# A hybrid diffusion trunk step on one core: the xBC and step-size projection in three rounded products

## The reference, cut to what matters

```
h = modulate(rmsnorm(x, n1), sh1, sc1)               # (384, 1024)
a_q,a_k,a_v, b_q,b_k,b_v, z, xbc, dt_raw = split(h @ w_in)   # w_in (1024, 2320)
xbc = silu(conv_centred(xbc, conv_w, conv_b))        # 768 columns, 3 taps along tokens
dt = softplus(dt_raw + dt_bias)                      # 16 columns
... attention of two kinds, Mamba-2 scan on xbc, dt, z -> o
x = x + g1 * (o @ w_out)
x = x + g2 * moe(modulate(rmsnorm(x, n2), sh2, sc2)) # 16 experts, top 2 in the top group
```

## Time and profile before

| | |
|---|---|
| runs | 819.34, 819.86, 821.42 us (median 819.86) |
| profiled execution | 819.76 us, its span 817.9 us |
| PE busy | 758.9 us, 93% of the span |
| DVE busy | 586.0 us, 72% |
| ACT busy | 476.9 us, 58% |
| chain that ended last | PE 79%, DVE 11%, ACT 5% |
| L825, plain product | 69.2 us in 192 records |

### The profile page before, as it was taken

How to read it: one execution, slowest core, us unless ns; L and a number is a source line. 1 busy time by engine, 2 the same in 40 slices (tenths; PEclk the granted TensorE clock), 3 DMA queues, 4 the chain that set the end, 5 groups by cost and what they waited for, 6 DMA issues and landing times.

```text
span 817.9 us, 10722 instructions
## 1 busy us (share of the span) xinstructions
PE 758.9 (93%) x3980; PEld 571.8 (70%) x3980; DVE 586.0 (72%) x934; ACT 476.9 (58%) x768; POOL 49.7 (6%) x36
## 2 busy tenths in 40 slices
PE   4997989999989999999989998988997799999995
PEld 2565878457945888888766787745793688888874
DVE  4229676884558789999663866688544988999965
ACT  3033883575355777777542388357534687777752
POOL 0000641000000000000000064100000000000000
PEclk9999999999999999999999999999998999999998
DMA  9952032978347899999760113285830179999912
GB/s 368 422 186 75 30 128 60 419 294 310 104 155 308 289 374 358 372 363 370 270 273 12 58 46 129 104 339 177 303 109 0 52 268 377 357 376 371 360 51 80
DMA packets 33488, 185.98 MB, mean 227 GB/s; under 512 B 5136, under 2 KB 6288, under 8 KB 16400
## 3 DMA queue, kind: packets, MB, share of 16 engines
q1 hardware_dynamic: 33424, 185.16, 60.2%
HBM read 182.53 MB, written 2.62 MB: 226 GB/s over the span
## 4 chain that ended last, share of the span: by engine, by line
PE 79%; DVE 11%; ACT 5%; issue 4%; DMA 1%; DVEq 0%; SPq 0%; ACTq 0%
PE psum L739 22%; PE psum L854 11%; PE psum L768 11%; PE psum L1056 8%; PE psum L825 7%; PE psum L791 3%; PE psum L620 2%; PE psum L1070 1%; DVE att L1930 1%; PE psum L817 1%; PE psum L924 1%; PE psum L717 1%; PE psum L1026 1%; PE psum L661 1%; PE psum L752 1%
## 5 line engine op out<-in xcount | busy, mean ns | idle before, releaser
L1726 DVE TENSOR_TENSOR split<-ring,split 128x2048 fp32r<-128x2048 f32 x96 | 219.9, 2291 | 27.6 <-ACT split L1319 25.0
L1319 ACT CAST split<-ring 128x2048 fp32r<-128x2048 f32 x96 | 183.4, 1911 | 18.1 <-PE psum L768 14.5
L739 PE MATMUL psum<-split,y_hi 128*128 128x512 f32 x512 | 162.7, 399 | 0.0
L739 PEld LDWEIGHTS psum<-split,y_hi 128*128 128x128 f32 x512 | 93.7, 188 | 19.6
L739 PE MATMUL psum<-split,y_lo 128*128 128x512 f32 x256 | 100.6, 393 | 0.0
L854 PE MATMUL psum<-ring_r,hT_hi 128*128 128x512 f32 x216 | 74.0, 397 | 2.7 <-ACT qkT L1413 2.4
L768 PE MATMUL psum<-split,hidT 128*128 128x512 f32 x256 | 70.3, 396 | 1.8 <-DVE hidT_lo L1731 1.8
L825 PE MATMUL psum<-hT,ring 128*128 128x384 f32 x192 | 69.2, 499 | 0.0
L768 PEld LDWEIGHTS psum<-split,hidT 128*128 128x128 f32 x256 | 47.4, 187 | 14.5 <-DVE hidT_lo L1731 3.6
L2120 POOL TENSOR_TENSOR ud<-const,da_hi 128x1024 fp32r<-128x1024 f32 x12 | 30.7, 2578 | 431.8 <-DVE da_lo L1823 431.3
L739 PEld LDWEIGHTS psum<-split,y_lo 128*128 128x128 f32 x256 | 48.0, 188 | 11.1
(11 more groups left out here) (258 smaller groups left out, 1339.0 us busy)
## 6 DMA issues: line engine op xcount, KB each, us to landing
ring<-in_w_gu SPq DMA_DIRECT2D x64, 1024.0 KB, 5.0
ring<-in_w_ada SPq DMA_DIRECT2D x40, 1024.0 KB, 6.7
ring<-in_w_down SPq DMA_DIRECT2D x32, 1024.0 KB, 5.2
ring<-in_w_rows SPq DMA_DIRECT2D x12, 1024.0 KB, 5.1
ring<-in_first SPq DMA_DIRECT2D x8, 1024.0 KB, 14.7
ring<-in_w_out SPq DMA_DIRECT2D x8, 1024.0 KB, 4.8
ring<-in_w_xbc SPq DMA_DIRECT2D x8, 784.0 KB, 8.4
par<-in_par SPq DMA_DIRECT2D x1, 1632.0 KB, 11.9
```

Of the source, the lines that this page charges most:

```text
L739: last = pe.matmul(dst, x[:, g, t, :], w[:, j, :], start=(t == 0 and i == 0), stop=(t == KD - 1 and i == 2))
L1319: act.copy(splits[n % SPLITS][:, 0, :], slot(key)).then_inc(raised("whi", l, p), 1)
L1726: tt(lo, slot(unit_key(l, p, n)), hi.bitcast(F32), ALU.subtract).then_inc(raised("wlo", l, p), 1)
```

## The change

The xBC and step-size product is made in three rounded products. Parts:

1. Per chunk 18 products (weight high x h high, weight rest x h high, weight high x h rest, for six groups) in place of 6 plain ones. Step sizes: h high against the 32 columns of dt_w (high and rest side by side), and h rest against the 16 high ones, six in place of three; VectorE adds the two results after the bias, one more add behind L1777.
2. The high part of x's pieces goes to new tiles x_hi and dt_w; the rest overwrites the piece. Pair 0 is split whole by VectorE at the start of the norm (the high part too), pairs 1 to 3 by ScalarE and VectorE in turn.
3. h is split chunk by chunk (`split_h`) within the norm in place of halves after it.
4. hT_hi has ring slots 2 and 3 for itself from the beginning of the stage: the h_hi entries stand first in the list, and the xbc pieces go elsewhere.
5. In layer 0 the casts of constant tables (`tables`) come after chunk 5, and the splits of w0 and w1 after chunk 6, both inside the norm; ScalarE's copies of the modulation rows are interleaved with the splits. w2 is split after the first convolution group. In layer 1 w0 and w1 are split after x3.

```diff
+IN_ORDER = (("x0", "h0", "h1", "x1", "h2", "h3", "x2", "h4", "h5", "x3", "h6", "w0", "w1", "h7", "w2", "w3", "w4", "w5"),
+            ("x0", "h0", "h1", "h2", "h3", "x1", "h4", "h5", "h6", "h7", "x2", "x3", "w0", "w1", "w2", "w3", "w4", "w5"))
...
-    s = [("norm", 0)] + ada[:early] + [("w_split", 0), ("h_split", 0), ("w_split", 1), ("h_split", 1), ("w_split", 2), ("xbc",)]
+    s = [("norm", 0)] + ada[:early] + [("xbc",)]
...
             if s[0] == "xbc":
+                pieces += [("h_hi", l, 0), ("h_hi", l, 1)]
                 if l == 0:
                     pieces.append(("first", 0, 0))
...
-        elif key[0] == "xbc" and key[2] < 2:
-            b = H_AT + 1 - key[2]
+        elif key[0] == "h_hi":
+            b = H_AT + key[2]
...
+        if key[0] == "h_hi":
+            last_use[b] = pieces.index(("w_hi", key[1], 5)) - 0.2 + 0.1 * key[2]
...
+                x_hi = sb("x_hi", [P, KD, XBC], F32R, c=ahead_of_masks)
+                dt_w = sb("dt_w", [P, KD, 2 * DT], F32R, c=ahead_of_masks)
...
 TensorE, kind "xbc"
-                            pe.wait_ge(*landed(("xbc", l, i)))
+                            pe.wait_ge(*in_lo(l, f"x{i}"))
                             for kk in range(2):
                                 k = 2 * i + kk
-                                pe.wait_ge(*modulated(l, 0, k))
+                                pe.wait_ge(*in_lo(l, f"h{k}"))
                                 for m in range(TILES):
-                                    last = pe.matmul(dtd[:, m * DT:(m + 1) * DT], hT[:, k, m * P:(m + 1) * P],
-                                                     w[:, kk, XBC:XBC + DT], start=(k == 0 and m == 0),
+                                    pe.matmul(dtd[:, 2 * m * DT:2 * (m + 1) * DT], hT_hi[:, k, tok], dt_w[:, k, :],
+                                              start=(k == 0 and m == 0), stop=(k == KD - 1), skip_group_check=True)
+                                    last = pe.matmul(dtd[:, 2 * m * DT:(2 * m + 1) * DT], hT_lo[:, k, tok], dt_w[:, k, 0:DT],
...
-                                    last = pe.matmul(bank(("xbc", l, c))[:, 0:TOK], w[:, kk, c * P:(c + 1) * P], hT[:, k, :],
-                                                     start=(k == 0), stop=(k == KD - 1))
+                                    for j, (w, x) in enumerate(((x_hi[:, k, part], hT_hi), (x_lo(l, i)[:, kk, part], hT_hi),
+                                                                (x_hi[:, k, part], hT_lo))):
+                                        last = pe.matmul(bank(("xbc", l, c))[:, 0:TOK], w, x[:, k, :],
...
 ScalarE
+            def split_x(l, i):
+                act.wait_ge(*landed(("xbc", l, i)))
+                act.copy(x_hi[:, 2 * i:2 * i + 2, :], src[:, :, 0:XBC])
+                act.copy(dt_w[:, 2 * i:2 * i + 2, 0:DT], src[:, :, XBC:XBC + DT]).then_inc(sig["in_hi"], 1)
+            def split_h(l, k):
+                act.wait_ge(*modulated(l, 0, k))
+                act.copy(hT_hi[:, k, :], hT[:, k, :]).then_inc(sig["in_hi"], 1)
...
 ScalarE, norm of layer 1 (c over all chunks; odd ones are modulated here)
+                    if not n:
+                        split_h(l, c)
+                        if c == 3:
+                            split_x(l, 1)
...
 ScalarE, kind "xbc"
                         if l == 0:
                             for j in range(KD):
                                 key = ("first", 0, j)
                                 act.wait_ge(*full(key))
                                 act.copy(ada_rows[:, 0:2 * P], bank(key)[:, 0:2 * P]).then_inc(*was_read(key))
+                                split_h(0, j)
+                                if j % 2 and j < KD - 1:
+                                    split_x(0, (j + 1) // 2)
+                                if j == KD - 2:
+                                    for p in range(2):
+                                        split_win(0, p)
...
+                        else:
+                            split_x(l, 2)
+                            split_x(l, 3)
+                        for p in range(0 if l else 2, 3):
+                            split_win(l, p)
...
 VectorE, norm
+                if l < DEPTH and not n:
+                    dve.wait_ge(*landed(("xbc", l, 0)))
+                    dve.tensor_copy(x_hi[:, 0:2, :], src[:, :, 0:XBC])
+                    dve.tensor_copy(dt_w[:, 0:2, 0:DT], src[:, :, XBC:XBC + DT]).then_inc(dve_step, 1)
+                    dve.wait_ge(dve_step, dve_steps())
+                    split_x(l, 0)
                 dve.wait_ge(sig["rstd"], 2 * l + n + 1)
...
+                    if l and not n and c0 == 1:
+                        split_h(l, 0)
...
+                        if not (l or n):
+                            split_h(0, c)
+                            if c % 2 and c < KD - 1:
+                                split_x(0, (c + 1) // 2)
+                            if c == KD - 3:
+                                tables()
+                            if c == KD - 2:
+                                for p in range(2):
+                                    split_win(0, p)
+                    if l and not n and c0:
+                        for c in range(c0, c1):
+                            split_h(l, c)
+                        for i in (1,) if c0 == 1 else (2, 3):
+                            split_x(l, i)
...
 VectorE, kind "xbc"
+                        for p in range(2 if l else 0):
+                            split_win(l, p)
...
+                        tt(dt_in, both[:, 0], bias, ALU.add).then_inc(dve_step, 1)
+                        dve.wait_ge(dve_step, dve_steps())
+                        tt(dt_in, both[:, 1], dt_in, ALU.add).then_inc(*was_read(key))
...
-                            if c == 2:
-                                dve.wait_ge(*release["xbc", l, KD // 2 - 1])
-                                split_h(l, 1, KD - 2, KD)
+                            if c == 0:
+                                split_win(l, 2)
```

More of the change, by code:

```diff
@@ L261, in build @@
                         pieces += [("first", 0, j) for j in (2 * i + 1, 2 * i + 2) if j < KD]
-                pieces += [("win", l, p) for p in range(5)] + [("w_hi", l, 2), ("win", l, 5), ("w_hi", l, 4), ("h_hi", l, 0),
-                                                               ("h_hi", l, 1), ("w_hi", l, 5)]
+                pieces += [("win", l, p) for p in range(5)] + [("w_hi", l, 2), ("win", l, 5), ("w_hi", l, 4), ("w_hi", l, 5)]
             elif s[0] == "ada":
@@ L404, in build @@
             cbd = sb("cbd", [P, 2], c=mix)
+            with ExitStack() as ahead_of_masks:
+                x_hi = sb("x_hi", [P, KD, XBC], F32R, c=ahead_of_masks)
+                dt_w = sb("dt_w", [P, KD, 2 * DT], F32R, c=ahead_of_masks)
             with ExitStack() as shared_late:
@@ L1229, in out_hi @@
                 act.copy(splits[out_split(n)][:, 0, :], slot(("wout", l, n))).then_inc(sig["mhi"], 1)
+            def split_x(l, i):
+                act.wait_ge(*landed(("xbc", l, i)))
+                src = slot(("xbc", l, i))[:, 0:2 * (XBC + DT)].rearrange("p (k n) -> p k n", k=2)
+                act.copy(x_hi[:, 2 * i:2 * i + 2, :], src[:, :, 0:XBC])
+                act.copy(dt_w[:, 2 * i:2 * i + 2, 0:DT], src[:, :, XBC:XBC + DT]).then_inc(sig["in_hi"], 1)
+            def split_h(l, k):
+                if k == 0:
+                    for i in range(2):
+                        if former_in["h_hi", l, i]:
+                            act.wait_ge(*release[former_in["h_hi", l, i]])
+                act.wait_ge(*modulated(l, 0, k))
+                act.copy(hT_hi[:, k, :], hT[:, k, :]).then_inc(sig["in_hi"], 1)
             def split_win(l, p):
@@ L1348, in _ @@
                         norm(l, arg[0])
-                        if not (l or arg[0]):
+                    elif kind == "ada" and arg[2] == KD - 1:
+                        ada(arg[0], arg[1])
+                    elif kind == "w_split":
+                        split_win(l, arg[0])
+                    elif kind == "xbc":
+                        if l == 0:
                             for j in range(KD):
```

98 lines of the change are left out of this document (46 added, 52 removed).

## The result

The changed kernel takes 826.94 us (median of 7 runs, 822.78 to 827.5), the kernel before 820.24 us on the same chip: ratio 1.0069, with a 95% interval of 1.005 to 1.0088. The change makes it 0.7% slower. The prediction was 809.3 us, range 803.5 to 816, with 0.89 for faster; it is wrong in sign. The profiled execution took 827.36 us (span 825.5, before 817.9).

What follows compares the result with a forecast made beforehand. TensorE's matmuls were taken to pace both products, except 4.29 us idle before layer 0's rows. From 819.8 us, less 6.9 in layer 0 and 3.6 in layer 1, came 809.3 us, range 803.5 to 816.

Steps and rivals of the forecast that it cites:

- Part 1: Product itself: wide fp32r products at 0.174 us, narrow ones at 0.095 us; a chunk takes 3.70 us in layer 1.
- Rival B: Both layers' products: narrow step products cost a wide one's 0.174 us each; 814 us; chance 0.08.
- Parts 2 to 4: Layer 0's feeding, ring and rows: product gains 1.3 us after 4.1 us of waits, rows start at 63.3; gain 6.9 us.
- Part 5: Layer 1's product: starts at 425.2, gains 6.7 us less waits of 1.7 and 1.4, ends at 456.4; gain 3.6 us.
- Rival D: Layer 0, chunk 5 into the rows: clock falls to half in waits; 30 us of it makes 824 us; chance 0.07.
- parts 3 to 5: Layer 0's ring and rows, layer 1's product: waits of 4.1 us in layer 0, 1.7 and 1.4 us in layer 1.
- the 4.29 us: Idle between product and first row product of layer 0 in the kernel before; the clock fall after it cost 1.3 us.
- Rival A: Feeding slower, above all in layer 0 around x3, w0, w1 and last modulation row: 812 to 814 us; chance 0.22.
- Rival C: Waits shorter in both layers as VectorE and ScalarE run ahead; all of 4.1 + 1.4 us back: 804 us; chance 0.12.
- Rival E: Rows wait for VectorE's convolution behind w2's split, both layers; 6 us of delay makes about 818 us; chance 0.06.
- Part 6: Layer 0's attention: nothing taken, bounds 0.9 us either way; experts, output product and end untouched.

Runs made afterwards that it cites:

- the combination with the root in SBUF: Changed kernel with layer 1's first norm root in SBUF, x0's split behind chunk 0's modulation in layer 1, and const and par loads moved: 818.04 us, 0.9968.
- the best version: the combination with the root in SBUF plus unread products on constants in TensorE's waits (5, 6, 7 in layer 0, 14 in layer 1): 814.24 us, 0.9916.
- the two edits of the norm's bank: Changed kernel, layer 1: multiply of chunks 4 to 7 ahead of x1's rest, 821.80 us; or instead reciprocal root written to SBUF, 820.47 us.
- the kernel before with its filler: Kernel before the change plus 16 products on constants in its one long wait, ahead of layer 0's rows: 819.23 us, ratio 0.9978.
- The changed kernel with fillers: Changed kernel plus unread products on constants in TensorE's waits (5, 6, 7 in layer 0, twice 18 in layer 1): 819.47 us, ratio 0.9979.
- the run with new table places: Changed kernel with const loaded behind x0 and par ahead of x2's wait in the first layer: 821.18 us, ratio 1.0025.

## Why the prediction was wrong, point by point

**Part 1, the price.** Nearly right. Wide products are 0.174 us apart at full clock. The narrow ones are 0.11 us apart instead of 0.095 (442.73, 442.87 and on), so a chunk takes 3.82 instead of 3.70 us in layer 1 and 5.48 instead of 5.34 us in layer 0: 1 us in each layer. Rival B is refuted.

**Parts 2 to 4, layer 0.** The sequence was right, the clock was not in it. Chunk 0 started at 20.14 us (19.2 foreseen) and took 7.87 us at half clock (5.34). x3 landed at 49.6 us (45.2), its casts and tables ended at 53.9 us (49.6). Chunks 6 and 7 started at 56.36 and 64.66 us (51.8 and 59.6), with the wait for the last modulation row as foreseen, 1.52 us for 1.7. The second wait, VectorE's 1.8 us, vanished, since chunk 6 ran at half clock and covered it. Chunk 7 took 6.06 us (3.7). The rows started at 70.72 instead of 63.3 us: of the 7.4 us, 2.4 are chunk 0's half clock, 2.2 chunk 7's, 0.9 the start, 1.1 the narrow products and the rest chunk 6, cold in its second half, less a wait. x3 was late because its load waits for the slot that chunk 3 uses last: it was issued at 44.62 us instead of 40.6, mostly since chunk 0's half clock had moved everything behind it. In the combination with the root in SBUF and without fillers, whose profiled execution (814.57 us, the shortest of its twelve) is at half clock for only 3.4 us of layer 0, inside chunk 6, chunks 6 and 7 and the rows start at 52.63, 60.46 and 64.38 us, within 1.1 us of the forecast, and the stage behind the rows is 6.05 us ahead of the kernel before; the forecast was 6.9.

**Part 5, layer 1.** Two steps failed besides the clock. "x0 is split by VectorE in the 4.88 us in which it waits for the norm; the 3.0 us cost nothing there": most of that wait is not free time, as the queue did not issue for 3.40 us of it, and the split started 0.7 us before the norm was ready. Start 427.73 instead of 425.2 us. And the multiply of chunks 4 to 7 was placed behind x1's rest without asking who waits for it; the part had no term for the norm's bank. The wait that was foreseen, 1.4 us ahead of chunk 4, did not come in the changed kernel, whose first two chunks were slow; in the best version, at full clock, it is there with 1.69 us (439.46). The sum: rows at 465.66 for 456.4 us, 9.3 us off. Start 2.5, narrow products 1.0, the bank's 1.53 us in place of 1.4, and 5.8 for the two chunks at half clock (15.0 us less the idle 1.53, where two chunks cost 7.6): 9.4 us.
The gain of 3.6 us was wrong even without the clock. In the best version, from the start of the norm's sums to the rows, it is 454.86 - 412.48 = 42.4 us; before it was 459.61 - 417.63 = 42.0 us. The product is 3.1 us shorter and starts 3.5 us later. What the change gave in these versions it gave in layer 0.

**Rival D, the step that decided.** "One fall cost 1.3 us"; "the gain is gone from 21 us at half clock on"; chance 0.07. The sum has no term for the clock: every wait of parts 3 to 5 is priced by its idle length, with the work behind it at full clock. The half clock in the three stretches is 6.8, 10.2 and 13.7 us, 30.7 us, about the figure at which D stood at 824 us; that D's figure was met is partly luck, since D placed all of it in layer 0, from chunk 5 on, and nearly half came in layer 1. With the two misses of layer 1 it made 827. What failed is the size and the chance, by one inference: the fall behind the 4.29 us was taken as the price of any fall. It hit a stage with no other idle. In layer 1 a second idle kept the clock down, as the two edits of the norm's bank show. In layer 0 it stayed down for 10.2 us with no idle behind the 1.52 us; why so long is not shown.
The Trainium skill has a case of this kind in "TensorE: Matmul & The Clock Gate", section HAM oscillation: a kernel that waits 3 to 5 us for its data between bursts goes back to the slow clock and pays at each wait. The trace of the changed kernel agrees for the 4.31 us, and shows 0.50 behind idles of 1.22 and 1.52 us too, shorter than that section's. The prediction read the section as speaking of waits of any length, and set it aside because the traces did not show it for such gaps; but the earlier trace rows did show a fall behind 1.82 us among other gaps.

**Rival A** was half true: the stretch with x3, w0 and w1 costs 1.7 to 3.6 us. **Rival C** did not occur: the wait ahead of chunk 7 went, but into slower work. **Rival E** did not occur in the changed kernel, there is no idle in its rows; it did where w0 and w1 were split behind chunk 7. **Part 6** missed 1.3 us in layer 1's attention, where the clock is 0.83 in 510 to 530 us against 1.00. This fall need not be the change's: the kernel before with its filler has one of the same length there, 505.1 to 511.9 us, and its attention is 1.3 us longer too (107.9 us from the end of the first rows to the output product, against 106.6). The changed kernel with fillers has no fall there, and 106.8 us.

**What stays open.** Why nearly the same idles are followed by a fall in one execution and not in another. Ahead of chunk 0 of layer 0 the run with new table places has idles of 0.41 and 1.03 us and the clock falls to 0.85 in 17.6 to 40 us; the combination with the root in SBUF has 0.41 and 1.03 us and stays at 1.00. The versions without fillers spread over 4 to 12 us, those with them over 5.5, 5.8 and, in 6 runs, 2.8 us. Also open is what holds VectorE's queue for 3.40 us: the branch is what the code has there. The Trainium skill, "Runtime: NRT & Kernel Launch", section Instruction fetch mechanics, says that a taken branch can stall the fetch of instructions. No run here moved the branch.

## What to carry to other kernels

In the kernel before, both products were paced by TensorE alone and ran at full clock. When such work is cut into shorter pieces that wait for other engines, price each wait by the chunks that then run at half clock, and not by its idle length, and ask whether the waits follow one another. Before a step is put into "free" time of a queue, look at what releases that idle (a semaphore or nothing that the profile names), and before work is put ahead of an instruction, find out who waits for the buffer it frees. Filler products on constants are a cheap probe: what they win back without making anything earlier is the clock's share.

## What the runs showed of the hardware that was not expected

- The clock went to 1.2 GHz for 6.8 us behind idles of 0.59 and 1.22 us (16 to 18 us), and for 10.2 us at one of 1.52 us (59.3 to 69.5 us), though the work that followed was dense. In the kernel before, idles of 0.59 and 0.42 us at the same place were followed by no fall, and 4.29 us had cost 1.3 us.
- Two idles, 4.31 and 1.53 us, 6.2 us of work apart, kept it down for 13.7 us; with the first alone it was back after 3.4 us in one version and 6.9 us in the other.
- Narrow fp32r products of 32 and 16 columns cost the same: 0.11 us each at full clock, 0.21 us at half clock.
- Fillers of 128 columns in fp32 take 0.24 us each (36 recorded passes in 4.29 us), and in layer 1 the product still started 9.83 us after the norm's sums, against 10.06 us without them.
